# Linear attention's last stage: the norms of three heads moved beside the fourth head's products

## The chip, the cores and the metric

The kernel runs on one core of one Trainium2 chip. The metric is the time of one execution on the device, in microseconds (us); less is better. A core has five engines that run side by side and wait for each other by semaphores: TensorE (PE in the profile, with its weight loads apart as PEld), VectorE (DVE), ScalarE (ACT), GpSimd (POOL) and SyncE (SP), which here only issues the weight transfers. TensorE writes to PSUM, which has eight banks of 512 float32 columns; the other three work from PSUM or SBUF.

## The reference

Two transformer blocks over 512 latent tokens and 256 context tokens, width 1024. The change concerns the first block's gated linear attention (GLA): 4 heads, key width 64, value width 128. What the stage at hand has to compute, from the reference:

```python
def merge_outputs(o_ret, o_gla, p, ret_norm_w, gla_norm_w, w_out, dtype):
    ...
    gl = merge_heads(o_gla * lax.rsqrt(jnp.mean(o_gla * o_gla, axis=-1, keepdims=True) + EPS))
    gl = gl * gla_norm_w * jax.nn.silu(p[7].astype(jnp.float32))
    return jnp.concatenate([r, gl], axis=-1).astype(dtype) @ w_out
```

Here `o_gla` is the sum of a forward and a backward scan. In the kernel each head's output is a product of its values with a 512 x 512 matrix of scores (the "own" products), plus a product of its decayed queries with the states that the context leaves behind (the "state" products), one for each direction. The rows of `w_out` that belong to GLA are applied after it, and the result is added to the residual `x` with a gate. The norm of the second feed-forward part follows.

## The kernel before

Everything is float32, laid out with features on the 128 partitions and tokens on the columns. Large products against weights are made in three passes: a weight is split into a high part `wh` (ScalarE, line 385) and a low part `wl` (VectorE, line 393), an activation likewise, and the passes high x high, high x low and low x high are added in PSUM. A float32 product without that split goes through TensorE in two passes, so one `matmul` of these shows as two records.

Each engine has its own instruction list, written out by hand in functions with the engine's name at their end (`gla_pe`, `gla_act`, `gla_dve`, `gla_pool`), and works through it in order. A `signal` is a counting semaphore: `.up(key)` goes with the instruction that raises it, `.at(key)` with the one that waits. `empty(pe, b)` makes TensorE wait until the last reader of bank b, noted in `emptied`, is done.

The end of the GLA stage, in the order of TensorE:

- Line 2149: the far parts of the score matrices, two bank halves for each head; ScalarE copies each into `W` (line 2258, printed `g_W`), in the order of the heads.
- `own_pe(h)`, line 2077: four products of 512 columns (eight passes) into bank 4+h, for heads 0 and 1 with the transposes of the decayed keys (line 2161) between them, then the context states (line 2171, banks 2 and 3; ScalarE copies them, line 2271), then heads 2 and 3. Before the first one TensorE waits for the last of ScalarE's copies into `W`.
- Line 2182: the state products of heads 0 to 3, two a head, contracting over 64 rows. Heads 0 and 2 lie on partitions 0 to 63, heads 1 and 3 on 64 to 127. They end the sum in bank 4+h and raise `gla_head`.
- ScalarE squares bank 4+h (line 2274, `g_sq`), then VectorE scales it by the norm's weight and the gate `gg` (line 2321, `g_g`).
- Line 2192: sums of the squares over features, as products with one column, four for each head (eight records), all 16 columns of the result in bank 0. Filler products (`idle_products`, line 473) whose result nobody reads stand between.
- One column step for all heads: mean plus epsilon (VectorE, line 2324), root (ScalarE, line 2277), reciprocal (VectorE, line 2326), then for each head a block of diagonal matrices of the factors (VectorE, line 2330, `g_dg`).
- Line 2200: a product with ones spreads each head's factors over the partitions, into bank h; four filler products follow.
- For each head VectorE multiplies by the factors (line 2334), ScalarE copies the product into the high part `gy` (line 2280, `g_y`), and the low part `gyl` (`g_yl`) is made by VectorE for heads 0 and 2 (line 2337) and by GpSimd for heads 1 and 3 (line 2351).
- `outproj_pe` with `by_features`, line 447: four chunks of `w_out`, each 256 output features from the 4 heads, 24 passes a chunk, banks 0 and 1 or 3 and 4. TensorE waits once for the low parts of heads 2 and 3. Within a chunk the first 128 output features come first, then the others. VectorE adds each half to `x` (line 1173), ScalarE squares it for the next norm (line 510), and both split the weights of the chunk after next between them.

The SyncE queue's transfers for this stage were issued before it, up to one at 966.85 us, and the next follows at 1032.41 us.

Of the kernel before, what the change touches and what calls it, by code (L numbers as in the profile page):

```python
# [6 lines left out]
EPS = 1e-6  # L7
# [233 lines left out]
def build(nc, wts, vec, con, conds, xin, cin, cin2, out):  # L241
# [5 lines left out]
    F32, F32R = mybir.dt.float32, mybir.dt.float32r  # L247
    ACT = mybir.ActivationFunctionType
    MUL, ADD, SUB, MAX, MIN = ALU.mult, ALU.add, ALU.subtract, ALU.max, ALU.min
# [60 lines left out]
    ones, ident, blk64, perm = (con0[:, 128 * i:128 * i + 128] for i in range(4))  # L310

    def V(n, i=0, w=1):
        return vecs[:, VEC[n][0] + i:VEC[n][0] + i + w]

    bank = [stack.enter_context(nc.psum_tensor(f"ps{i}", [128, 512], F32)) for i in range(8)]
# [86 lines left out]
    emptied = [None] * 8  # L402

    def empty(pe, *banks):
        for b in banks:
            if emptied[b]:
                s, key = emptied[b]
                pe.wait_ge(*s.at(*key))
                emptied[b] = None
# [59 lines left out]
    def idle_products(pe, b, n):  # L469

        empty(pe, b)
        for _ in range(n):
            pe.matmul(bank[b][:, :], ones, con0[:, :], start=True, stop=True, skip_group_check=True)  # L473
# [1438 lines left out]
    gla_spread = signal("gla_spread")  # L1912
    gla_done = signal("gla_done")

    def outproj_pe(pe, name, k0, yh, yl, ready, ctx, key, between=None):
        for m in range(4):
            b = SETS[m % 2]
            if m == 0:
                ready(pe)
            by_features(pe, W_OF[name, k0, 256 * m], b, yh, yl, True, ctx)  # L1920
            for i in range(3 if ctx else 2):
                emptied[b[i]] = resid, (key, 0, m, i)
            if between:
                between(m)
# [27 lines left out]
    def tiles_of(t):  # L1952
        return t.rearrange("p (j n) -> p j n", j=4)
# [117 lines left out]
        emptied[6] = consumer, ("narrow", 0)  # L2071
        emptied[7] = consumer, ("narrow", C)

    def own_pe(pe, h):
        empty(pe, 4 + h)
        for jt in range(4):
            pe.matmul(bank[4 + h][:, :], gv[:, 2 + jt, 128 * h:128 * h + 128], W[:, h, jt, :], start=jt == 0, stop=False, skip_group_check=True)

    FAR = ((0, 1), (1, 0), (2, 3), (3, 2))

    def gla_pe(pe):
        narrow_pe(pe, w_in(GR), rank)
# [11 lines left out]
        def ready(pe):  # L2094
            pe.wait_ge(*y_low_pool.at("r", 3))
# [32 lines left out]
        for s in (7, 8):  # L2128
# [4 lines left out]
            for h in range(4):  # L2133
# [9 lines left out]
                else:  # L2143
                    for half in range(2):
# [5 lines left out]
                                          qq[:, 256 - 256 * half:512 - 256 * half], start=True, stop=True, skip_group_check=True)  # L2150
                        i.then_inc(*far.up(8, h, half))
                        emptied[bb] = far_out, (8, h, half)
        pe.wait_ge(*far_out.at(8, 3, 1))
        pe.wait_ge(*values_out.at("g", 5))
        own_pe(pe, 0)
        for d in range(2):
# [16 lines left out]
            i.then_inc(*gla_state.up(d))  # L2173
            emptied[bb] = gla_state_out, (d,)
        own_pe(pe, 2)
        own_pe(pe, 3)
        pe.wait_ge(*gla_state_out.at(1))
        pe.wait_ge(*query_decayed.at(1))
        for h in range(4):
            hp, r0 = h // 2, 64 * (h % 2)  # L2180
            for d in range(2):
                i = pe.matmul(bank[4 + h][:, :], stt[r0:r0 + 64, d, hp, 128 * (h % 2):128 * (h % 2) + 128], qs[d][r0:r0 + 64, hp, :],
                              start=False, stop=d == 1, skip_group_check=True)
            i.then_inc(*gla_head.up(h))
            emptied[4 + h] = gla_scaled, (h,)
        empty(pe, 0)
        for h in range(4):
            if h == 1 or h == 2:
                idle_products(pe, 1, 1)
            pe.wait_ge(*gla_sq.at(h))  # L2190
            for i in range(4):
                j = pe.matmul(bank[0][:, 4 * h + i:4 * h + i + 1], gsq[:, h, 128 * i:128 * i + 128], ones[:, 0:1], start=True, stop=True,
                              skip_group_check=True)
        j.then_inc(*sums_out.up("g"))
        emptied[0] = rstd, ("g", 0)
        idle_products(pe, 1, 1)
        for h in range(4):
            empty(pe, h)
            pe.wait_ge(*gla_diag.at(h))
            pe.matmul(bank[h][:, :], ones, gdg[:, 512 * h:512 * h + 512], start=True, stop=True,  # L2200
                      skip_group_check=True).then_inc(*gla_spread.up(h))
            emptied[h] = gla_done, (h,)
        idle_products(pe, 6, 4)

        def ready(pe):
            pe.wait_ge(*y_low.at("g", 2))
            pe.wait_ge(*y_low_pool.at("g", 3))

        outproj_pe(pe, "w_out", 4, Lat(gy), Lat(gyl), ready, False, "gla")

    def gla_act(act):

# [56 lines left out]
        for d in range(2):  # L2269
            act.wait_ge(*gla_state.at(d))  # L2270
            act.activation(stt[:, d, :, :], bank[2 + d][:, :].rearrange("p (j n) -> p j n", j=2), ACT.Copy).then_inc(*gla_state_out.up(d))
        for h in range(4):
            act.wait_ge(*gla_head.at(h))
            act.activation(gsq[:, h, :], bank[4 + h][:, :], ACT.Square).then_inc(*gla_sq.up(h))
        c = cb[:, 0:3, :].rearrange("p a b -> p (a b)")[:, 0:16]
        act.wait_ge(*rstd.at("g", 0))
        act.activation(c, c, ACT.Sqrt).then_inc(*root.up("g"))
        for h in range(4):
            act.wait_ge(*gla_done.at(h))
            act.activation(gy[:, h, :], gg[:, h, :], ACT.Copy).then_inc(*y_high.up("g", h))  # L2280

        outproj_act(act, "w_out", 4, lambda m: None, norm3, lambda e, k: e.wait_ge(*resid.at("gla", "x", k)))

    def gla_dve(dve):
# [31 lines left out]
        for d in range(2):  # L2316
            dve.wait_ge(*key_exp.at(d))
            dve.tensor_tensor(kx[:, d, :, :], kx[:, d, :, :], kk[:, :, CTX], MUL).then_inc(*key_decayed.up(d))
        for h in range(4):
            dve.wait_ge(*gla_sq.at(h))  # L2320
            dve.scalar_tensor_tensor(gg[:, h, :], bank[4 + h][:, :], V("gla_norm_w", h), gg[:, h, :], MUL, MUL).then_inc(*gla_scaled.up(h))
        c = cb[:, 0:3, :].rearrange("p a b -> p (a b)")[:, 0:16]
        dve.wait_ge(*sums_out.at("g"))
        dve.tensor_scalar(c, bank[0][:, 0:16], 1.0 / 128, EPS, MUL, ADD).then_inc(*rstd.up("g", 0))
        dve.wait_ge(*root.at("g"))
        dve.reciprocal(c, c).then_inc(*rstd.up("g"))
        dve.wait_ge(*rstd.last())
        shp = [128, 4, 128]
        for h in range(4):
            dve.tensor_tensor(tiles_of(gdg[:, 512 * h:512 * h + 512]), ident.unsqueeze(1).broadcast_to(shp),  # L2330
                              c[:, 4 * h:4 * h + 4].unsqueeze(2).broadcast_to(shp), MUL).then_inc(*gla_diag.up(h))
        for h in range(4):
            dve.wait_ge(*gla_spread.at(h))
            dve.tensor_tensor(gg[:, h, :], gg[:, h, :], bank[h][:, :], MUL).then_inc(*gla_done.up(h))
            if h % 2 == 0:
                dve.wait_ge(*y_high.at("g", h))
                dve.tensor_tensor(gyl[:, h, :], gg[:, h, :], gy[:, h, :].bitcast(F32), SUB).then_inc(*y_low.up("g", h))
        outproj_dve(dve, "w_out", 4, lambda k, s: M1[:, 40 + k, s:s + 1], False, "gla", lambda m: None, norm3)

    def gla_pool(pool):  # L2340
# [1703 lines left out]
```

## Time and profile before

| | us |
|---|---|
| median of 3 runs | 2681.16 |
| lowest and highest | 2677.81, 2688.44 |
| the profiled execution, its own time | 2678.36 |
| its span, first to last instruction | 2676.6 |

| engine | busy, share of the span |
|---|---|
| TensorE | 2590.9 us, 97% |
| VectorE | 1289.2 us, 48% |
| ScalarE | 820.4 us, 31% |
| GpSimd | 221.3 us, 8% |

The mean granted clock of TensorE over the span is 0.983 of full speed. The chain of work that ended last has 87% of its time on TensorE. The stage that the change touches lies between some 976 and 1029 us of the span. Busy shares here are shares of time in which a record of the engine is open; TensorE's matmuls overlap, so their starts tell the pace, and a busy TensorE may be doing fillers.

### The profile page before, as it was taken

The page shows a single profiled execution, that of the slowest core. Times are in us where ns is not written, and L with a number is a line of the kernel's source. Part 1 is how long each engine was busy: PE and PEld are TensorE (multiplying, and loading weights), DVE is VectorE, ACT ScalarE, POOL GpSimd, SP SyncE. Part 2 cuts the span into 40 slices and gives each one's busy share as a digit, 9 for nine tenths or more (in the row PEclk, how much of TensorE's full clock was granted, in tenths as well). Part 3 has the DMA queues.
Part 4 walks back from the last instruction along what each step waited for, and adds up shares of the span by engine and source line. Part 5 has one row for each costly group of instructions (what it writes and reads, how often), then busy time and mean ns, then how long its engine had stood idle before and what let it go on. Part 6 is the DMA issues. An engine that isn't in the chain of part 4 may idle for free.

```text
span 2676.6 us, 30609 instructions
## 1 busy us (share of the span) xinstructions
PE 2590.9 (97%) x12874; PEld 2039.6 (76%) x12874; DVE 1289.2 (48%) x1978; ACT 820.4 (31%) x1180; POOL 221.3 (8%) x176
## 2 busy tenths in 40 slices
PE   7999999999999999999999999999999999999998
PEld 4888888888756766888887686787788688686666
DVE  6564434336345745667647522522332342476562
ACT  3211112134333243222224313122222312245663
POOL 0100000021110000000000020110210011110001
PEclk9999999999999899999999999999999999999999
DMA  7344333312102002455532110110021011011010
GB/s 281 118 153 145 136 136 110 111 48 95 56 25 79 8 24 79 159 183 177 176 125 77 57 40 17 68 51 32 32 79 48 16 65 62 32 65 64 32 48 32
DMA packets 45401, 223.54 MB, mean 84 GB/s; under 512 B 4768, under 2 KB 6992, under 8 KB 30672
## 3 DMA queue, kind: packets, MB, share of 16 engines
q1 hardware_dynamic: 43296, 215.24, 22.8%
q10 hardware_dynamic: 1968, 6.34, 0.7%
q8 instruction: 102, 1.67, 0.2%
q14 instruction: 35, 0.29, 0.0%
HBM read 219.46 MB, written 2.10 MB: 83 GB/s over the span
## 4 chain that ended last, share of the span: by engine, by line
PE 87%; DVE 6%; ACT 4%; issue 2%; POOL 1%; DMA 0%; SPq 0%; POOLq 0%; DVEq 0%; ACTq 0%
PE ps L447 41%; PE ps L444 12%; PE ps L1513 7%; PE ps L422 3%; PE ps L3344 3%; PE ps L2892 3%; PE ps L867 1%; PE ps L1236 1%; PE ps L3552 1%; ACT wh L385 1%; PE ps L3456 1%; DVE wl L393 1%; PE ps L2710 1%; PE ps L3576 1%; PE ps L473 1%
## 5 line engine op out<-in xcount | busy, mean ns | idle before, releaser
L393 DVE TENSOR_TENSOR wl<-stage,wh 128x2048 fp32r<-128x2048 f32 (+2 forms) x157 | 326.2, 2078 | 633.1 <-ACT wh L385 632.9
L447 PE MATMUL ps<-hh,wh 128*128 128x512 f32 x1152 | 456.5, 396 | 0.0
L447 PE MATMUL ps<-hl,wh 128*128 128x512 f32 x1152 | 455.7, 396 | 0.0
L447 PE MATMUL ps<-hh,wl 128*128 128x512 f32 x1152 | 455.3, 395 | 0.0
L385 ACT ACTIVATE wh<-stage 128x2048 fp32r<-128x2048 f32 (+2 forms) x157 | 267.5, 1704 | 532.5 <-PE ps L447 387.0
L447 PEld LDWEIGHTS ps<-hh,wh 128*128 128x128 f32 x1152 | 217.8, 189 | 50.7 <-issue 1.2
L447 PEld LDWEIGHTS ps<-hh,wl 128*128 128x128 f32 x1152 | 217.4, 189 | 50.3
L447 PEld LDWEIGHTS ps<-hl,wh 128*128 128x128 f32 x1152 | 217.4, 189 | 49.1 <-issue 1.2
L641 DVE CUSTOM_DVE_ANT_0 left<-direct,cond_rows,vecs 128x1024 bf16<-128x1024 f32 x168 | 207.0, 1280 | 0.0
L444 PE MATMUL ps<-hh,wh 128*128 128x256 f32 x688 | 196.0, 285 | 4.0 <-DVE r_tb L1643 2.8
L444 PE MATMUL ps<-hh,wl 128*128 128x256 f32 x688 | 194.9, 283 | 0.0
L444 PE MATMUL ps<-hl,wh 128*128 128x256 f32 x688 | 193.8, 282 | 0.0
L444 PEld LDWEIGHTS ps<-hh,wh 128*128 128x128 f32 x688 | 131.9, 192 | 8.0 <-issue 4.3
L444 PEld LDWEIGHTS ps<-hl,wh 128*128 128x128 f32 x688 | 131.2, 191 | 0.0
L444 PEld LDWEIGHTS ps<-hh,wl 128*128 128x128 f32 x688 | 131.1, 191 | 0.0
L1513 PE MATMUL ps<-wh,hh 128*128 128x512 f32 x288 | 119.9, 416 | 0.0
L1513 PE MATMUL ps<-wh,hl 128*128 128x512 f32 x288 | 116.1, 403 | 0.0
L1513 PE MATMUL ps<-wl,hh 128*128 128x512 f32 x288 | 115.7, 402 | 0.0
L1191 POOL TENSOR_TENSOR ul<-sl,uh 128x768 fp32r<-128x768 f32 (+1 forms) x28 | 43.7, 1573 | 853.7 <-ACT uh L1082 853.4
L1082 ACT ACTIVATE uh<-sl 128x512 fp32r<-128x512 f32 (+1 forms) x42 | 30.8, 734 | 229.3 <-DVE sl L1142 138.2
L447 PE MATMUL ps<-uh,wh 128*128 128x512 f32 x240 | 94.3, 393 | 0.0
L447 PE MATMUL ps<-ul,wh 128*128 128x512 f32 x240 | 94.3, 393 | 0.0
(594 smaller groups left out, 4663.3 us busy)
## 6 DMA issues: line engine op xcount, KB each, us to landing
stage<-wts SPq DMA_DIRECT2D x108, 1024.0 KB, 4.8
direct<-wts SPq DMA_DIRECT2D x104, 512.0 KB, 4.2
stage<-wts SPq DMA_DIRECT2D x24, 768.0 KB, 4.3
stage<-wts SPq DMA_DIRECT2D x26, 512.0 KB, 3.3
group<-wts SPq DMA_DIRECT2D x6, 512.0 KB, 6.4
first<-wts SPq DMA_DIRECT2D x6, 512.0 KB, 9.7
x<-xin SPq DMA_DIRECT2D x4, 512.0 KB, 7.4
group<-wts SPq DMA_DIRECT2D x2, 1024.0 KB, 9.4
```

The source lines that it names most:

```text
L385: act.activation(split(m)[0][:, 0:w], stage[m % 2][:, 0:w], ACT.Copy).then_inc(*w_high.up(m))
L393: dve.tensor_tensor(l[:, 0:w], stage[m % 2][:, 0:w], h[:, 0:w].bitcast(F32), SUB).then_inc(*w_low.up(m))
L422: i = pe.matmul(bank[b[f]][:, :], w[:, k, 128 * f:128 * f + 128], s[:, k, LAT], start=k == 0 and a == 0, stop=k == nk - 1 and a == 2, skip ...
L444: i = pe.matmul(bank[b[2]][:, 256 * f:256 * f + 256], w[:, k, cols], s[:, k, CTX], start=st, stop=en, skip_group_check=True)
L447: i = pe.matmul(bank[b[f]][:, :], w[:, k, cols], s[:, k, LAT], start=st, stop=en, skip_group_check=True)
L473: pe.matmul(bank[b][:, :], ones, con0[:, :], start=True, stop=True, skip_group_check=True)
L641: dve.tensor_tensor_reduce(left[n % 2][:, :], chunk[:, :], rows_of[:, s, :], 1.0, bias[:, s:s + 1], MUL, ADD, to[:, s:s + 1]).then_inc(*mo ...
L1082: act.activation(z.uh[:, k, z.lo:T], z.sl[(2 * p + f) % 4][:, z.lo:T], ACT.Copy).then_inc(*u_high.up(n, p, f))
L1191: pool.tensor_tensor(z.ul[:, k, z.lo:T], z.sl[(2 * p + f) % 4][:, z.lo:T], z.uh[:, k, z.lo:T].bitcast(F32), SUB).then_inc(*u_low_pool.up(n ...
L1513: i = pe.matmul(bank[t][:, :], s[:, 4 * j + k, 128 * t:128 * t + 128], u[:, k, :], start=j == 0 and k == 0 and a == 0, stop=j == 1 and k = ...
L2892: pe.matmul(bank[b[0]][:, :], mv_[:, J, fs], wpart(J, C, T), start=J == 0, stop=J == 5, skip_group_check=True)
L3344: i = pe.matmul(bank[f][:, :], u[:, k, 128 * f:128 * f + 128], s[:, k, LAT], start=k == 0 and a == 0, stop=k == 7 and a == 2, skip_group_c ...
```

## The change

- `own_pe(0)` waits for ScalarE's copies into `W` of head 0, `own_pe(h)` for those of head h; the wait for head 3's ahead of all is gone. `own_pe` can be given some of its four products.
- State products of heads 0, 1 and 2 come right after the own products of head 2. Then two of head 3's four own products, the sums of heads 0 to 2 (bank 3), head 3's other two, its state products, the spread of head 0, the sums of head 3 (bank 2), the spreads of heads 1 and 2.
- The column step and the diagonals are done twice, for heads 0 to 2 and for head 3 (`NORM_HEADS`).
- A head's factors are spread into its own bank 4+h. All filler products of this stretch are gone.
- The first chunk of the projection uses the other branch of `by_features`: group k (head k's six passes, over both output halves) after a wait for the low part of head k. The spread of head 3 stands between groups 0 and 1. Both halves of the chunk are ready at its end.
- ScalarE's and VectorE's lists are put in the order that goes with it; head 0's product, high and low part stand in the middle of head 3's column step.

The diff:

```diff
-    def outproj_pe(pe, name, k0, yh, yl, ready, ctx, key, between=None):
+    def outproj_pe(pe, name, k0, yh, yl, ready, ctx, key, between=None, tile_ready=None):
         for m in range(4):
             b = SETS[m % 2]
-            if m == 0:
+            if m == 0 and ready:
                 ready(pe)
-            by_features(pe, W_OF[name, k0, 256 * m], b, yh, yl, True, ctx)
+            by_features(pe, W_OF[name, k0, 256 * m], b, yh, yl, True, ctx, tile_ready if m == 0 else None)
...
-    def own_pe(pe, h):
-        empty(pe, 4 + h)
-        for jt in range(4):
+    def own_pe(pe, h, jts=range(4)):
+        if jts[0] == 0:
+            pe.wait_ge(*far_out.at(8, h, 1))
+            empty(pe, 4 + h)
+        for jt in jts:
             pe.matmul(bank[4 + h][:, :], gv[:, 2 + jt, 128 * h:128 * h + 128], W[:, h, jt, :], start=jt == 0, stop=False, skip_group_check=True)
...
+    NORM_HEADS = ((0, 3), (3, 4))
...
-        pe.wait_ge(*far_out.at(8, 3, 1))
         pe.wait_ge(*values_out.at("g", 5))
         own_pe(pe, 0)
...
         own_pe(pe, 2)
-        own_pe(pe, 3)
         pe.wait_ge(*gla_state_out.at(1))
         pe.wait_ge(*query_decayed.at(1))
-        for h in range(4):
+
+        def from_states(h):
             hp, r0 = h // 2, 64 * (h % 2)
...
-        empty(pe, 0)
-        for h in range(4):
-            if h == 1 or h == 2:
-                idle_products(pe, 1, 1)
-            pe.wait_ge(*gla_sq.at(h))
-            for i in range(4):
-                j = pe.matmul(bank[0][:, 4 * h + i:4 * h + i + 1], gsq[:, h, 128 * i:128 * i + 128], ones[:, 0:1], start=True, stop=True,
-                              skip_group_check=True)
-        j.then_inc(*sums_out.up("g"))
-        emptied[0] = rstd, ("g", 0)
-        idle_products(pe, 1, 1)
-        for h in range(4):
-            empty(pe, h)
+
+        def sums(heads, n):
+
+            empty(pe, 3 - n)
+            for h in heads:
+                pe.wait_ge(*gla_sq.at(h))
+                for i in range(4):
+                    j = pe.matmul(bank[3 - n][:, 4 * h + i:4 * h + i + 1], gsq[:, h, 128 * i:128 * i + 128], ones[:, 0:1], start=True, stop=True,
+                                  skip_group_check=True)
+            j.then_inc(*sums_out.up("g", n))
+            emptied[3 - n] = rstd, ("g", n, 0)
+
+        def spread_head(h):
+
+            empty(pe, 4 + h)
             pe.wait_ge(*gla_diag.at(h))
-            pe.matmul(bank[h][:, :], ones, gdg[:, 512 * h:512 * h + 512], start=True, stop=True,
+            pe.matmul(bank[4 + h][:, :], ones, gdg[:, 512 * h:512 * h + 512], start=True, stop=True,
                       skip_group_check=True).then_inc(*gla_spread.up(h))
-            emptied[h] = gla_done, (h,)
-        idle_products(pe, 6, 4)
-
-        def ready(pe):
-            pe.wait_ge(*y_low.at("g", 2))
-            pe.wait_ge(*y_low_pool.at("g", 3))
-
-        outproj_pe(pe, "w_out", 4, Lat(gy), Lat(gyl), ready, False, "gla")
+            emptied[4 + h] = gla_done, (h,)
+
+
+        for h in range(3):
+            from_states(h)
+        own_pe(pe, 3, range(2))
+        sums(range(3), 0)
+        own_pe(pe, 3, range(2, 4))
+        from_states(3)
+        spread_head(0)
+        sums((3,), 1)
+        for h in (1, 2):
+            spread_head(h)
+
+        def tile_ready(c, k):
+            if c == 0 and k == 1:
+                spread_head(3)
+            pe.wait_ge(*(y_low_pool if k % 2 else y_low).at("g", k))
+
+        outproj_pe(pe, "w_out", 4, Lat(gy), Lat(gyl), None, False, "gla", None, tile_ready)
...
+        for n, (h0, h1) in enumerate(NORM_HEADS):
+            for h in range(h0, h1):
+                act.wait_ge(*gla_head.at(h))
+                act.activation(gsq[:, h, :], bank[4 + h][:, :], ACT.Square).then_inc(*gla_sq.up(h))
+            if n:
+                gla_high(0)
+            act.wait_ge(*rstd.at("g", n, 0))
+            act.activation(c[:, 4 * h0:4 * h1], c[:, 4 * h0:4 * h1], ACT.Sqrt).then_inc(*root.up("g", n))
+        for h in range(1, 4):
+            gla_high(h)
...
+        for n, (h0, h1) in enumerate(NORM_HEADS):
+            for h in range(h0, h1):
+                dve.wait_ge(*gla_sq.at(h))
+                dve.scalar_tensor_tensor(gg[:, h, :], bank[4 + h][:, :], V("gla_norm_w", h), gg[:, h, :], MUL, MUL).then_inc(*gla_scaled.up(h))
+            if n:
+                gla_done_dve(0)
+            cc = c[:, 4 * h0:4 * h1]
+            dve.wait_ge(*sums_out.at("g", n))
+            dve.tensor_scalar(cc, bank[3 - n][:, 4 * h0:4 * h1], 1.0 / 128, EPS, MUL, ADD).then_inc(*rstd.up("g", n, 0))
+            if n:
+                gla_low_dve(0)
+            dve.wait_ge(*root.at("g", n))
+            dve.reciprocal(cc, cc).then_inc(*rstd.up("g", n))
+            dve.wait_ge(*rstd.last())
+            for h in range(h0, h1):
+                dve.tensor_tensor(tiles_of(gdg[:, 512 * h:512 * h + 512]), ident.unsqueeze(1).broadcast_to(shp),
+                                  c[:, 4 * h:4 * h + 4].unsqueeze(2).broadcast_to(shp), MUL).then_inc(*gla_diag.up(h))
+        gla_done_dve(1)
+        gla_done_dve(2)
+        gla_low_dve(2)
+        gla_done_dve(3)
```

`gla_done_dve(h)` is line 2334's product (now from bank 4+h), `gla_low_dve(h)` line 2337's low part, `gla_high(h)` line 2280's copy; GpSimd's list is as it was.

## Rows read from the trace of the kernel before

**Rows 1.** The page's first line.

```profile
span 2676.6 us, 30609 instructions
```

**Rows 2.** The chain that ended last, 980 to 1040 us: start us, us, what.

```profile
980.75 0.61 ACT g_W L2258
...
1020.48 2.40 issue
1022.88 17.05 PE ps L447 x72
```

**Rows 3.** Timeline, TensorE and VectorE, 958 to 989 us: idle before in brackets.

```profile
976.00 4.71 PE L2149 MATMUL ps<-g_qs,g_qs 64*128 64x256 f32 x16 [2.26 <-ACT g_W L2258]
981.40 6.61 PE L2077 MATMUL ps<-g_W,g_v 128*128 128x512 f32 x8 [0.69 <-ACT g_W L2258]
...
981.89 1.29 DVE L2318 TENSOR_TENSOR g_kx<-g_kx,g_k 128x512 f32<-128x512 f32 x2 [8.77 <-ACT g_kx L2262]
```

**Rows 4.** Windows: us, PE, PEld, DVE, ACT, POOL busy, clock, DMA share, GB/s.

```profile
977.00:980.40 3.40, 3.40 (x13) 2.61 (x11) 0.00 (x0) 1.98 (x4) 0.00 (x0) 0.51 0.00 0
...
983.80:987.20 3.40, 3.40 (x5) 1.35 (x4) 0.00 (x0) 0.47 (x1) 3.40 (x2) 0.50 0.00 0
...
1007.80:1011.20 3.40, 3.40 (x25) 2.68 (x23) 0.54 (x1) 0.89 (x1) 0.00 (x0) 1.00 0.00 0
...
1018.00:1021.40 3.40, 2.48 (x6) 0.76 (x4) 2.08 (x3) 1.48 (x3) 1.26 (x1) 1.00 0.00 0
```

**Rows 5.** Timeline, TensorE and its weight loads, 992 to 1028 us.

```profile
995.61 7.03 PE L2077 MATMUL ps<-g_W,g_v 128*128 128x512 f32 x16
1002.57 3.81 PE L2182 MATMUL ps<-g_qs,g_st 64*128 64x512 f32 x16
...
1009.91 1.84 PE L2192 MATMUL ps<-con,g_sq 128*128 128x1 f32 x16
...
1003.53 0.20 PEld L2182 LDWEIGHTS ps<-g_qs,g_st 64*128 64x128 f32 x2 [0.23 <-issue]
```

**Rows 6.** Timeline, VectorE, ScalarE and GpSimd, 992 to 1028 us.

```profile
1004.59 1.09 ACT L2274 ACTIVATE g_sq<-ps 128x512 f32<-128x512 f32 x2 [8.18 <-PE ps L2182]
1005.22 1.41 DVE L2321 SCALAR_TENSOR_TENSOR g_g<-ps,vecs,g_g 128x512 f32<-128x512 f32 x2 [22.03 <-ACT g_sq L2274]
1007.41 1.28 ACT L2277 ACT_TABLE_LOAD   x1
1011.79 0.17 DVE L2324 TENSOR_SCALAR cb<-ps 128x16 f32<-128x16 f32 x1 [3.45 <-PE ps L2192]
1012.25 0.25 DVE L2326 RECIPROCAL cb<-cb 128x16 f32<-128x16 f32 x1 [0.28 <-ACT cb L2277]
1012.54 2.50 DVE L2330 TENSOR_TENSOR g_dg<-con,cb 128x512 f32<-128x512 f32 x4
1014.95 0.68 DVE L2334 TENSOR_TENSOR g_g<-g_g,ps 128x512 f32<-128x512 f32 x1
1015.67 0.63 ACT L2280 ACTIVATE g_y<-g_g 128x512 fp32r<-128x512 f32 x1 [3.45 <-DVE g_g L2334]
1016.33 0.69 DVE L2337 TENSOR_TENSOR g_yl<-g_g,g_y 128x512 fp32r<-128x512 f32 x1 [0.70 <-ACT g_y L2280]
1018.36 1.26 POOL L2351 TENSOR_TENSOR g_yl<-g_g,g_y 128x512 fp32r<-128x512 f32 x1 [30.30 <-ACT g_y L2280]
1018.91 1.26 DVE L2337 TENSOR_TENSOR g_yl<-g_g,g_y 128x512 fp32r<-128x512 f32 x1 [0.70 <-ACT g_y L2280]
...
1021.51 1.26 POOL L2351 TENSOR_TENSOR g_yl<-g_g,g_y 128x512 fp32r<-128x512 f32 x1 [1.89 <-ACT g_y L2280]
1026.73 0.63 ACT L510 ACTIVATE n_acc<-x 128x512 f32<-128x512 f32 x1 [5.30 <-DVE x L1173]
```

**Rows 7.** Timeline, ScalarE and VectorE, 1028 to 1042 us: the next weights' split.

```profile
1030.07 1.04 ACT L385 ACTIVATE wh<-stage 128x1024 fp32r<-128x1024 f32 x1
...
1031.15 1.23 DVE L393 TENSOR_TENSOR wl<-stage,wh 128x1024 fp32r<-128x1024 f32 x1 [0.26 <-ACT wh L385]
```

More of the change, by code:

```diff
@@ L2271, in gla_act, with gla_high @@
             act.activation(stt[:, d, :, :], bank[2 + d][:, :].rearrange("p (j n) -> p j n", j=2), ACT.Copy).then_inc(*gla_state_out.up(d))
-        for h in range(4):
-            act.wait_ge(*gla_head.at(h))
-            act.activation(gsq[:, h, :], bank[4 + h][:, :], ACT.Square).then_inc(*gla_sq.up(h))
         c = cb[:, 0:3, :].rearrange("p a b -> p (a b)")[:, 0:16]
-        act.wait_ge(*rstd.at("g", 0))
-        act.activation(c, c, ACT.Sqrt).then_inc(*root.up("g"))
-        for h in range(4):
+        def gla_high(h):
             act.wait_ge(*gla_done.at(h))
             act.activation(gy[:, h, :], gg[:, h, :], ACT.Copy).then_inc(*y_high.up("g", h))
+        for n, (h0, h1) in enumerate(NORM_HEADS):
[8 more added lines that the diff above has]
+            gla_high(h)
         outproj_act(act, "w_out", 4, lambda m: None, norm3, lambda e, k: e.wait_ge(*resid.at("gla", "x", k)))
@@ L2318, in gla_dve @@
             dve.tensor_tensor(kx[:, d, :, :], kx[:, d, :, :], kk[:, :, CTX], MUL).then_inc(*key_decayed.up(d))
-        for h in range(4):
-            dve.wait_ge(*gla_sq.at(h))
-            dve.scalar_tensor_tensor(gg[:, h, :], bank[4 + h][:, :], V("gla_norm_w", h), gg[:, h, :], MUL, MUL).then_inc(*gla_scaled.up(h))
         c = cb[:, 0:3, :].rearrange("p a b -> p (a b)")[:, 0:16]
-        dve.wait_ge(*sums_out.at("g"))
-        dve.tensor_scalar(c, bank[0][:, 0:16], 1.0 / 128, EPS, MUL, ADD).then_inc(*rstd.up("g", 0))
@@ L2325, in gla_dve, with gla_done_dve @@
-        dve.wait_ge(*root.at("g"))
-        dve.reciprocal(c, c).then_inc(*rstd.up("g"))
-        dve.wait_ge(*rstd.last())
         shp = [128, 4, 128]
[L2329 to L2332, printed above, removed]
+        def gla_done_dve(h):
             dve.wait_ge(*gla_spread.at(h))
[L2334 to L2337, printed above, removed]
+            dve.tensor_tensor(gg[:, h, :], gg[:, h, :], bank[4 + h][:, :], MUL).then_inc(*gla_done.up(h))
@@ new lines, in gla_low_dve @@
+        def gla_low_dve(h):
+            dve.wait_ge(*y_high.at("g", h))
+            dve.tensor_tensor(gyl[:, h, :], gg[:, h, :], gy[:, h, :].bitcast(F32), SUB).then_inc(*y_low.up("g", h))
+        for n, (h0, h1) in enumerate(NORM_HEADS):
[15 more added lines that the diff above has]
+                                  c[:, 4 * h:4 * h + 4].unsqueeze(2).broadcast_to(shp), MUL).then_inc(*gla_diag.up(h))
```

## The prediction

> **What bounds the kernel now.** First the page: one core, 2676.6 us of span, 2678.36 us as its own time (1.8 us lie around the span) [rows 1]. The median of the runs shown, 2681.16, is 2.8 us above the profiled execution. The change touches some 40 us, so I read only the end of linear attention: first the chain of work there, then TensorE alone, then the granted clock, then the other engines.
>
> The chain is TensorE nearly everywhere; what it does at the end, though, is not all work. After the last state product (from 1002.57) the projection starts at 1022.88 [rows 2, 5]. In these 20.3 us TensorE has 3.8 us of state products, 32 one-column sums, eight passes that spread the factors and seven filler products of two passes each that nobody reads. It then stands for 2.40 us before line 447 [rows 2]. The view calls that "issue", but VectorE's last product of head 3, ScalarE's copy and GpSimd's low part precede it, and the low part ends at 1021.51 + 1.26 = 1022.77 [rows 6]. So the bound is the dependent chain of head 3, not TensorE: the fillers are free time, and work put into it costs nothing.
>
> Unit prices on TensorE: a 512-column float32 pass goes off each 7.03/16, about 0.43 us, at full clock [rows 5], and each 0.85 at 1.2 GHz (6.61 us for eight, the last faster) [rows 3]. A one-column sum with its load takes 1.78/16, 0.11 us [rows 5]. A projection pass takes 17.05/72, 0.235 us, so a chunk of 24 takes 5.6 [rows 2]. Sixteen state passes took only 3.8 us, loads going in twos [rows 5]: heads 0 and 1, on rows 0 to 63 and 64 to 127, run beside each other, and so do 2 and 3. A pair costs 1.8 us; a head without its partner also costs 1.72 (four passes of 0.43).
>
> **The change part by part.** All times are those of before's trace, without the earlier start that the first part brings.
>
> *The wait ahead of the first own product.* It was for the last copy of head 3, 980.75 + 0.61, and the products began at 981.40 [rows 2, 3]. They now need head 0's copies only, long done. TensorE's last line-2149 pass ends at 980.7 and the next could go off at about 980.5, so they start 0.9 us earlier. The clock was at 1.2 GHz from 977 to past 987.2 [rows 4]. Had it come back at the same moment, the 0.9 us would be worth half, 0.45. Had it come back by 983.8 because the dense work starts earlier, 3.4 us more of it run at double pace: 0.9 + 1.7 = 2.6. If it comes back as long after the first product as before, the gain is 0.9, which I take. Nothing behind is in the way: VectorE's products for the transposes end at 981.89 + 1.29 = 983.2 [rows 3], and TensorE comes to them near 987.
>
> *The order of TensorE.* Head 2's own products start at 995.61 and take 3.4, to 999.1. Now head 3's eight follow only later. Heads 0 and 1 take their state products at 999.1 to 1000.95, head 2 alone to 1002.7. Then come four own passes of head 3 (1.7) to 1004.45, 24 sums of 0.11 (2.7) to 1007.2, four own passes to 1008.95, and head 3's state products alone to 1010.75. Splitting the pair 2 and 3 costs 1.7 us, and it stands on the path.
>
> *Norms of heads 0 to 2.* A square starts 2.0 us after its pair's first pass [rows 5, 6]: 1001.15, and head 2's at 1002.85, done 1003.45; VectorE's scalings of 0.75 follow. Both are ahead of the sums at 1004.45. The table load of 1.28 [rows 6], which stood under the sums, now starts at 1003.45 and is over by 1004.75, before the root at 1007.6. Sums out 1007.4, column step 0.17, root 0.2, reciprocal 0.25, diagonals of 0.6 each [rows 6]: head 0's factor is ready at 1008.7, head 2's at 1010. TensorE comes to head 0's at 1010.75, so all of it is hidden under head 3's products. That is what the change gains.
>
> *Head 3.* Its state products land 1.9 after their start, at 1010.9; square to 1011.5; TensorE spreads head 0 meanwhile (0.86) and then does eight sums, 1011.6 to 1012.5. VectorE has scaling (to 1012.2), head 0's product (to 1012.9), the column step, head 0's low part, which waits for ScalarE's copy of 0.63 (1013.6 to 1014.3), reciprocal (to 1014.5) and the diagonal (to 1015.2). Would the square after the root need a second table load? Line 510's square runs after the root and no load stands ahead of it [rows 6]; no. If it did, twice 1.28 at most.
>
> *The projection's inputs.* TensorE spreads heads 1 and 2 to 1014.25, and group k=0 (six passes, 1.4) starts with the low part of head 0, 1014.35 to 1015.75. Head 3's spread, ready since 1015.2, takes until 1016.6. VectorE's products of heads 1 and 2 end at 1015.8 and 1016.4. ScalarE's copy of head 1 ends at 1016.45, GpSimd's low part at 1017.8. So k=1 starts at 1017.9: a wait of 1.3 us on TensorE. Head 2's low part on VectorE, due at 1017.1 and behind it head 3's product, takes either 0.69 (as at 1016.33) or waits for GpSimd: the one that ran beside GpSimd's operation, at 1018.91, took 1.26 and ended 0.55 after it [rows 6]. I take the second, since it falls beside one here too: low part at 1018.35, head 3's product 1018.9, copy 1019.6, GpSimd's low part 1020.9. k=2 runs from 1019.3 to 1020.7, k=3 from 1021.0 to 1022.4. Before, the chunk ran 1022.88 + 5.6 = 1028.5. **Gain 6.1 us**; with the part ahead **7.0 us**. With the free low part (0.69) it would be 7.3.
>
> The Trainium skill (SBUF — State Buffer, "Who interferes with whom") says that a VectorE instruction with two SBUF inputs and a GpSimd instruction that reads SBUF shut each other out, the second waiting until the first has ended. The row at 1018.91 agrees (0.55 us after GpSimd's end), and by the rule the gain is the 7.0, not the 7.3. By it, too, an instruction of VectorE that came first would hold GpSimd's low part of head 1 back instead; VectorE's products of heads 1 to 3 have one input in PSUM and would not.
>
> *The loop order of the first chunk.* Both halves of the output now end with the chunk, not 2.8 us apart. Two additions of 0.75, two squares of 0.63, and the high part (1.04) and low part (1.23) of the chunk after next queue up behind it. Before, that low part ended at 1032.38, 3.9 after the chunk [rows 7]; I work out 4.8 now (additions to 1.8, second square to 2.4, high part to 3.5). The chunk between takes 5.6, so it is hidden with 0.8 us to spare. Were it not, only the excess would count.
>
> *Banks.* The spreads go into banks 4 to 7, free once the scalings are done (head 3's at 1012.2, spread at 1015.75); the sums into 3 and 2, which ScalarE has copied out before any state product starts. The fourteen fillers are gone, for which the clock is the only price.
>
> The rest is bound by TensorE in the same order, so I pass the 7.0 us on whole: 2678.36 - 7.0 = 2671.4 against the profiled execution, 2681.16 - 7.0 = 2674.2 against the median. I take 2673.
>
> **The rivals.**
> *A, the forecast*: 0.62, 2673 us, on its own 2669 to 2677.
>
> *B, the clock falls in the sums.* The 24 one-column sums run together for 2.7 us, with no filler between. For: a stretch with 2.26 us of standing at 973.7 [rows 3] led to 1.2 GHz from 977 on [rows 4]. Against: at 1007.8 to 1011.2 two thirds were such sums, with fillers, and at 1018 to 1021.4 TensorE stood for 0.9 us, and the clock held [rows 4]. The price, if it falls at 1007.2 and stays some 10 us as at 977: eight passes of head 3 cost 0.43 more each (3.4), the spreads and k=0 some 1.5 on the path; 5 in all. Gain 2, so 2678. Chance 0.18.
> The Trainium skill (TensorE: Matmul & The Clock Gate, "A second HAM failure mode: psum-queue depth-cycling") tells of kernels whose TensorE stands briefly between groups that go around the banks, and whose clock therefore swings between its levels. That rule speaks for B; the rows at 1007.8 and 1018 have such short stops at full clock, so I leave B the minor case.
>
> *C, the clock returns earlier at the own products.* 2.6 in place of 0.9 for the first part: 2671. Chance 0.12.
>
> *D, head by head doesn't pay.* A late low part of head 1 (a GpSimd operation held back by 0.7, or VectorE's queue holding head 2's product behind a late diagonal) makes TensorE stand at k=1 and then at k=3, as it now does once. Each us late there costs one; with 3 us late 2676. Chance 0.05.
>
> *E, slower.* The clock falls in the sums and stays down through the whole projection, since k=0 to k=3 wait between groups. A chunk of 24 passes then takes 24 x 0.43 = 10.2 instead of 5.6; four cost 18.5 more, with B's 5 it is 23.5, minus 7: 2695. It becomes slower than before from 14 us at 1.2 GHz on, each costing half, and by over 0.5% from 41 us on. In this stage the longest such stretch was 10 us [rows 4], and the later chunks run with no wait. Chance 0.03.
>
> **How the numbers follow.** 0.5%, 13.4 us, is about what a measurement of this kernel can tell from no change: the three runs shown lie from 2677.81 to 2688.44. No case gains 13.4; A to D all lie within 0.5%. The scatter of the medians can add some 5 us to C or A, which gives faster 0.05; E gives slower 0.03; the rest, 0.92, is the same. The range reaches from C less the scatter, 2666, to B with it, 2682.
>
> **What would show it.** The first own product some 0.9 us sooner after the last line-2149 pass. Twenty-four one-column sums in a row with head 3's passes on both sides, and no fillers. From the start of head 2's own products to the start of the second chunk some 26.8 us instead of 32.9. A stop of about 1.3 us ahead of k=1, and VectorE's low part of head 2 near 1.2 us. The granted clock at full speed from 1007 to 1018 shows A; 1.2 GHz there shows B. I am wrong if head 3's diagonal is not ready behind k=0, if a second table load stands there, or if the chunk after next waits for its low part.

## The result, and the profile after

The changed kernel takes 2670.47 us (median of 20 runs, 2664.19 to 2679.4) against 2681.84 (20 runs, 2673.49 to 2690.83): a ratio of 0.996, 95% interval 0.9949 to 0.997, or 8 to 14 us less. In a second measurement (the run e10 below) it was 0.996 again (0.9948 to 0.9973). The forecast of 2673 is 2.5 us above this median; the gain worked out for it, 7.0 us, lies just under the interval. The profiled executions: 2669.46 us with a span of 2667.7, before 2678.36 with 2676.6.

What an execution does ahead of the stage varies more than the change is worth: the second run of line-2149 passes starts at 976.00 before, at 977.40 and 981.22 in two executions of the changed kernel, and at 971.19 in the run e1 below, with the same instructions ahead. So I compare stretches between marks, the first mark being that start. The **first stretch** goes from there to the start of head 2's own products, the **second** to the first pass of the projection's second chunk, the **third** to the first pass of the second feed-forward, and the **rest** to the end.

| us | first | second | third | rest | sum |
|---|---|---|---|---|---|
| before | 19.6 | 32.9 | 28.2 | 1619.9 | 1700.6 |
| after | 17.5 | 27.0 | 28.7 | 1617.0 | 1690.3 |
| forecast | 18.7 | 26.8 | 28.2 | 1619.9 | 1693.6 |

The timeline of the changed kernel, TensorE (answers to [rows 3, 5]; the own products are now line 2079, the sums 2195, the state products 2184, the spreads 2204; in the first chunk line 422 is the head-by-head branch, k=1 its six passes of head 1):

```profile
977.40 4.75 PE L2152 MATMUL ps<-g_qs,g_qs 64*128 64x256 f32 x16 [2.27 <-ACT g_W L2274]
982.08 5.24 PE L2079 MATMUL ps<-g_W,g_v 128*128 128x512 f32 x8
...
994.92 3.60 PE L2079 MATMUL ps<-g_W,g_v 128*128 128x512 f32 x8
998.45 3.70 PE L2184 MATMUL ps<-g_qs,g_st 64*128 64x512 f32 x12
1002.08 1.98 PE L2079 MATMUL ps<-g_W,g_v 128*128 128x512 f32 x4
1003.90 2.73 PE L2195 MATMUL ps<-con,g_sq 128*128 128x1 f32 x24
1006.50 1.96 PE L2079 MATMUL ps<-g_W,g_v 128*128 128x512 f32 x4
1008.39 1.98 PE L2184 MATMUL ps<-g_qs,g_st 64*128 64x512 f32 x4
...
1017.24 0.50 PE L422 MATMUL ps<-g_y,wh 128*128 128x512 f32 x1 [0.83 <-POOL g_yl L2388]
...
1021.92 0.40 PE L447 MATMUL ps<-g_y,wh 128*128 128x512 f32 x1
```

The own products no longer wait (no bracket), and take 5.24 us, not 6.61. The order from 994.92 on is the one forecast, each piece within 0.2 us. The one stop over 0.5 us is at k=1, for GpSimd, 0.83 us. The same kernel's windows (columns as in [rows 4]):

```profile
978.40:985.20 6.80, 6.80 (x17) 4.17 (x16) 1.29 (x2) 4.99 (x9) 0.35 (x1) 0.50 0.00 0
...
1003.80:1006.60 2.80, 2.80 (x26) 2.70 (x25) 0.00 (x0) 0.28 (x1) 0.00 (x0) 1.00 0.00 0
1006.60:1018.00 11.40, 10.57 (x34) 5.22 (x34) 7.90 (x15) 2.76 (x6) 1.26 (x1) 1.00 0.00 0
...
1043.20:1046.60 3.40, 3.40 (x6) 1.34 (x5) 2.79 (x5) 0.21 (x1) 0.00 (x0) 0.51 0.81 248
```

Beside the own products TensorE was at 1.2 GHz for 6.8 us, where before it stayed there from 977 to past 987.2 [rows 4]. It held 2.4 GHz through the sums and the first chunk. At norm 3 it fell for 3.4 us, which it had not done before; that is the 0.6 us by which the third stretch is longer. Over all fourteen traces the third stretch is 28.7 us in the nine that have this fall and 28.2 in the five that don't (before, e1, e4, e6, e11). The low parts, VectorE and GpSimd (answers to [rows 6]):

```profile
1015.92 1.26 POOL L2388 TENSOR_TENSOR g_yl<-g_g,g_y 128x512 fp32r<-128x512 f32 x1 [26.40 <-ACT g_y L2292]
1019.07 1.29 POOL L2388 TENSOR_TENSOR g_yl<-g_g,g_y 128x512 fp32r<-128x512 f32 x1 [1.89 <-ACT g_y L2292]
...
1016.47 1.26 DVE L2351 TENSOR_TENSOR g_yl<-g_g,g_y 128x512 fp32r<-128x512 f32 x1 [0.70 <-ACT g_y L2292]
```

Head 2's low part started 0.55 us after GpSimd's operation and took 1.26 us, as forecast. The Trainium skill (SBUF — State Buffer, "Who interferes with whom") has the second of the two wait for the end of the first; VectorE ended 0.55 us after GpSimd, as before. GpSimd's operations here read and write SBUF alone: in no trace does a row of it name `ps`.

### The profile page after: what moved, and what is told of

Same layout as the page of the kernel before. It is cut to its first block, busy times and chain, and to the rows that moved or that the text cites. A ratio compares the mean times of both kernels' runs of the same rounds, so it can differ in the third digit from the quotient of the medians.

```text
span 2667.7 us, 30589 instructions
## 1 busy us (share of the span) xinstructions
PE 2585.7 (97%) x12860; PEld 2036.5 (76%) x12860; DVE 1289.0 (48%) x1980; ACT 820.9 (31%) x1181; POOL 221.4 (8%) x176
## 4 chain that ended last, share of the span: by engine, by line
PE 87%; DVE 7%; ACT 4%; issue 2%; POOL 1%; DMA 0%; SPq 0%; POOLq 0%; DVEq 0%; ACTq 0%
PE ps L447 41%; PE ps L444 12%; PE ps L1513 7%; PE ps L422 3%; PE ps L3381 3%; PE ps L2929 3%; PE ps L867 1%; PE ps L3589 1%; PE ps L1236 1%; PE ps L3493 1%; PE ps L2747 1%; ACT wh L385 1%; PE ps L473 1%; PE ps L3613 1%; DVE wl L393 1%
```

## The experiments

All with one trace each; ratios are to the kernel before, of 8 to 12 executions against 30 to 36 of the kernel before in the same measurement, with 95% intervals.

| run | first | second | third | rest | ratio |
|---|---|---|---|---|---|
| e1, before + early start | 17.5 | 33.0 | 28.2 | 1619.1 | 0.9979 (0.9968 to 0.999) |
| e2, after, old wait | 19.6 | 28.6 | 28.7 | 1621.1 | 0.9995 (0.9985 to 1.0005) |
| e3, after, one wait for all | 17.5 | 33.8 | 28.7 | 1620.8 | 0.9998 (0.9986 to 1.0011) |
| e4, after + fillers | 17.5 | 28.7 | 28.2 | 1619.6 | 0.9974 (0.9962 to 0.9986) |
| e5, low parts swapped | 17.5 | 26.4 | 28.7 | 1617.9 | 0.9956 (0.9942 to 0.997) |
| e6, before, no fillers | 19.6 | 33.2 | 28.2 | 1620.4 | 1.0 (0.9988 to 1.0012) |
| e7, before + by head | 19.6 | 28.8 | 28.7 | 1624.2 | 0.999 (0.998 to 1.0) |
| e9, heads in pairs | 17.5 | 27.4 | 28.7 | 1623.6 | 0.9972 (0.9957 to 0.9986) |
| e10, after again | 17.5 | 27.0 | 28.7 | 1621.0 | 0.996 (0.9948 to 0.9973) |
| e11, one low part on GpSimd | 17.5 | 26.0 | 28.2 | 1625.6 | 0.9956 (0.994 to 0.9973) |
| e12, pairs, none on GpSimd | 17.5 | 24.7 | 28.7 | 1620.2 | 0.996 (0.9947 to 0.9974) |
| e13, e2 + fillers | 19.6 | 28.7 | 28.7 | 1627.1 | 0.9989 (0.9978 to 1.0001) |

**e1, the early start alone.**

```diff
     def own_pe(pe, h):
+        pe.wait_ge(*far_out.at(8, h, 1))
         empty(pe, 4 + h)
...
-        pe.wait_ge(*far_out.at(8, 3, 1))
```

> The kernel before, with only the first part of the change: each head's own products wait for that head's copies. Two stretches are compared: the first from the second run of line-2149 passes to the start of head 2's own products (before 19.6 us, after the change 17.5), the second from there to the start of the projection's second chunk (before 32.9, after 27.0). Theory 1 (the start alone, clock as it falls): own products 0.9 us earlier, first stretch 18.7 on average over the clock's moments, the time 0.9 us shorter. Theory 2 (the earlier start regularly brings the clock back sooner): first stretch 17.5, the time 2.1 shorter. Both: second stretch unchanged at 32.9.

First stretch 17.5: theory 2. The own products of head 0 after it, at 1.2 GHz for 6.8 us:

```profile
972.80:979.60 6.80, 6.80 (x14) 3.30 (x11) 1.29 (x2) 4.90 (x8) 1.56 (x1) 0.50 0.00 0
979.60:983.00 3.40, 3.40 (x15) 1.97 (x14) 0.00 (x0) 1.08 (x2) 3.10 (x2) 0.99 0.00 0
```

In all nine traces with the early start this stretch is 17.5 us, in all five without it 19.6. The time was 3 to 9 us shorter, more than the 2.1 of theory 2; the section on the prediction comes back to that.

The second stretch stayed at 33.0 although the clock fell in it, which it had not done before. All fillers were in place, and the stop ahead of the spreads was the 0.65 us that before has too. Timeline and window:

```profile
1006.50 5.37 PE L2200 MATMUL ps<-g_dg,con 128*128 128x512 f32 x8 [0.65 <-DVE g_dg L2330]
...
1016.07 0.47 PE L447 MATMUL ps<-g_y,wh 128*128 128x512 f32 x1 [0.77 <-issue]
```

```profile
1007.00:1010.40 3.40, 3.40 (x5) 1.35 (x4) 2.70 (x5) 0.63 (x1) 0.00 (x0) 0.50 0.00 0
```

It cost nothing, because TensorE waits at the end of this stretch: its stop ahead of line 447 was 0.77 us in place of 2.40.

**e2, the changed kernel with the old wait.**

```diff
+        pe.wait_ge(*far_out.at(8, 3, 1))
         pe.wait_ge(*values_out.at("g", 5))
         own_pe(pe, 0)
```

> The changed kernel with the old wait put back: TensorE waits for ScalarE's last copy of head 3 ahead of the first own product. Theory 1: first stretch longer by 0.9 than with the change, 18.4 to 19.6 by the clock's moment; the time 0.9 longer than the changed kernel's. Theory 2: first stretch back at 19.6, 2.1 longer. Both: second stretch 27.0 as with the change.

First stretch back at 19.6, but the second is 28.6, which neither theory had. The timeline and the windows of this run:

```profile
1005.76 2.73 PE L2196 MATMUL ps<-con,g_sq 128*128 128x1 f32 x24
1008.36 3.08 PE L2079 MATMUL ps<-g_W,g_v 128*128 128x512 f32 x4
```

```profile
1005.60:1009.10 3.50, 3.50 (x27) 3.06 (x26) 0.29 (x2) 0.56 (x2) 0.00 (x0) 1.00 0.00 0
1009.10:1012.50 3.40, 3.40 (x5) 0.96 (x4) 2.00 (x4) 0.00 (x0) 0.00 (x0) 0.50 0.00 0
```

The clock fell for 3.4 us behind the 24 sums: rival B's mechanism, at 1.6 us. In the changed kernel it did not in either trace, nor in e3, e5 and e11, which have the same 24 sums and the early start. What differs in e2 is the wait ahead of the own products and, with it, when the clock had last risen.

**e13, e2 with fillers among the sums**, to see whether the sums did it.

```diff
             for h in heads:
+                if h == 1 or h == 2:
+                    idle_products(pe, 1, 1)
                 pe.wait_ge(*gla_sq.at(h))
```

> The changed kernel with the old wait (the run e2) and two filler products among the sums of heads 0 to 2. In e2 TensorE fell to 1.2 GHz at the end of the 24 sums and the second stretch took 28.6; in the changed kernel, with the earlier start, it did not and took 27.0. Theory 4 (the fall comes from sums without a filler at that moment): no fall here, second stretch 27.0 + 1.7 = 28.7, the time about that of e2. Rival (the fall has another cause): a fall again and 30.3. First stretch 19.6.

28.7 and no fall, over the same windows:

```profile
1005.60:1009.10 3.50, 3.50 (x22) 2.54 (x21) 0.00 (x0) 0.17 (x1) 0.00 (x0) 1.00 0.00 0
1009.10:1012.50 3.40, 3.40 (x15) 1.92 (x14) 2.11 (x5) 0.21 (x1) 0.00 (x0) 1.00 0.00 0
```

The forecast of theory 4 came true: with fillers among the sums, no fall. Theory 4 is still not the whole rule: e1 has fillers among its sums and fell at 1007.0, the changed kernel has none and did not. Each side of this comparison is one trace, and the fillers also move all that follows by 1.7 us. Fillers cost what the fall costs (1.7 against 1.6).

**e4, the changed kernel with the same fillers.**

> The changed kernel with two filler products (four passes) put back among the sums of heads 0 to 2. If TensorE is what bounds this part, as forecast: second stretch 27.0 + 1.9 = 28.9. If what follows has slack there: 27.0. If the clock sometimes falls without them, this kernel is the steadier one.

28.7: TensorE is on the path here, and with the early start there was no fall for them to prevent.

**e6, the kernel before without fillers**: the seven products of `idle_products` in this stretch taken out.

> The kernel before without the seven filler products of this stretch. If the fillers were free and the clock holds without them: the two among the sums stood on the path (about 0.97 us each), the others did not, so the second stretch is 32.9 - 1.9 = 31.0 and the time 1.9 shorter. If they held the clock up (the mechanism of rival B): 1.2 GHz somewhere between the sums and the first chunk, second stretch 33 or more.

33.2, the second case. The clock was at 1.2 GHz twice, behind the 32 sums and at the first chunk:

```profile
1009.20:1012.60 3.40, 3.04 (x4) 1.51 (x5) 2.70 (x5) 0.24 (x1) 0.00 (x0) 0.50 0.00 0
1019.40:1022.80 3.40, 3.24 (x8) 2.59 (x9) 0.00 (x0) 0.00 (x0) 0.06 (x1) 0.51 0.00 0
```

The seven fillers of before together paid for themselves (32.9 with them). Which of them kept the clock up where isn't separated here.

**e7, the head-by-head projection alone**: `tile_ready` with its waits and the spreads in banks 4+h, put into the kernel before; the last four fillers out.

> The kernel before with the head-by-head projection, the heads' own banks for the factors and without the four last fillers; the order of the norms stays as it was. By the rows of before, k=0 starts at 1017.1, k=1 after GpSimd at 1019.7, k=3 at 1022.8, the second chunk at 1024.3 in place of 1028.5: second stretch 28.7, 4.2 of the 5.9 us. If instead the norms beside head 3 carry the gain: second stretch above 31. First stretch as before.

28.8: 4.2 of the 5.9 us. The other 1.8 come with two things at once: the norms beside head 3's products, and without the three fillers that e7 still has, of which the two among the sums stand on the path. e4 has the new order of the norms with these two fillers and takes 28.7. So with them in place the new order is worth 0.1 us against e7; it hides work, but it also pays 1.7 us for the split pair. The 1.8 come from the fillers that can go, and whether e7's order would keep 2.4 GHz without them no run shows; the order of before did not (e6).

**e3, the changed kernel with one wait for all low parts.**

```diff
+        spread_head(3)
...
-        outproj_pe(pe, "w_out", 4, Lat(gy), Lat(gyl), None, False, "gla", None, tile_ready)
+        outproj_pe(pe, "w_out", 4, Lat(gy), Lat(gyl), ready, False, "gla")
```

> The changed kernel, but the projection waits once for all four low parts and its first chunk takes the old loop order; head 3's spread stands ahead of it. The chunk then starts when GpSimd has made head 3's low part, about 1020.4 in the changed kernel's times, perhaps 0.3 sooner: second chunk 4 us later, second stretch 31 and the time 4 longer than the changed kernel's. If the head-by-head order is worth little: under 29.

33.8, 6.8 more, not 4, and 0.9 more than the kernel before. TensorE stood 4.60 us (timeline), the clock fell, and the chunk ran its first 5.7 us at 1.2 GHz (windows):

```profile
1017.97 0.77 PE L447 MATMUL ps<-g_y,wh 128*128 128x512 f32 x1 [4.60 <-issue]
```

```profile
1016.90:1023.70 6.80, 5.73 (x14) 4.50 (x15) 0.23 (x1) 0.00 (x0) 0.97 (x1) 0.50 0.00 0
```

At 2.4 GHz these 5.7 us would have taken about half, an estimate of 2.9 us less or 30.9, which is the 31 expected. So the norms beside head 3 gain nothing behind one wait without fillers, for two reasons: the wait itself, and the low clock that it brings. Fillers under this wait, as the kernel before had them, were not tried; by the estimate they might leave 2 us of gain.

**e5, low parts swapped**: VectorE makes those of heads 1 and 3, GpSimd those of 0 and 2.

> The changed kernel with the low parts given the other way round: heads 0 and 2 to GpSimd, heads 1 and 3 to VectorE. Theory (VectorE's queue and GpSimd's two low parts end the chain now): k=0 starts 0.5 later, k=1 has no wait, k=3 needs VectorE's 0.7 in place of GpSimd's 1.3: second chunk 1.1 us earlier, second stretch 25.9. Rival (TensorE's passes bound it, low parts have slack): 27.0 or, with the later k=0, 27.5.

26.4, half way. No wait at k=1, but TensorE stood for 0.49 us ahead of k=0, for GpSimd's low part of head 0, and VectorE's diagonal of head 3, which started under that operation, took 1.54 us in place of 0.69:

```profile
1014.63 1.26 POOL L2387 TENSOR_TENSOR g_yl<-g_g,g_y 128x512 fp32r<-128x512 f32 x1 [23.75 <-ACT g_y L2292]
...
1014.90 1.54 DVE L2367 TENSOR_TENSOR g_dg<-con,cb 128x512 f32<-128x512 f32 x1
```

**e11, only head 2's low part on GpSimd.**

> The changed kernel with the low parts of heads 0, 1 and 3 on VectorE and that of head 2 alone on GpSimd. Theory (the two waits of TensorE in the first chunk are GpSimd's 1.3 us): no wait at k=1, VectorE's diagonal and low part of head 0 undisturbed, second chunk at 25.9 in place of 27.0. Rival (VectorE becomes the bound): 26.5 or more. The time 1 us shorter than the changed kernel's, if the clock falls in the same places.

26.0, within 0.1 of what was worked out. The stop at k=1 was 0.23 us, for VectorE's low part, in place of 0.83.

**e9, heads 2 and 3 as a pair**: `NORM_HEADS` is ((0, 2), (2, 4)); three of head 3's four own products ahead of the sums of heads 0 and 1, one behind; the spreads of heads 2 and 3 between k=0 and k=1.

> The changed kernel with the norms split in twos: heads 0 and 1 beside head 3's own products, state products of heads 2 and 3 as a pair again, the spreads of heads 2 and 3 between k=0 and k=1. Theory (splitting the pair costs 1.7 us on the path): the pair's passes take 1.8 for both, second chunk 1.5 us earlier, second stretch 25.5. Rival (head 2's norm, now late, costs as much as the pair saves): 27 or more.

27.4. The clock fell between k=0 and k=1:

```profile
1010.70:1014.10 3.40, 3.40 (x8) 1.99 (x7) 1.32 (x3) 0.58 (x1) 1.82 (x1) 0.50 0.00 0
```

and GpSimd's low part of head 1, which started while VectorE's diagonals ran, took 1.82 us in place of 1.26; at k=3 TensorE stood 0.94 us for GpSimd again:

```profile
1010.76 1.29 DVE L2371 TENSOR_TENSOR g_dg<-con,cb 128x512 f32<-128x512 f32 x2
...
1011.36 1.82 POOL L2389 TENSOR_TENSOR g_yl<-g_g,g_y 128x512 fp32r<-128x512 f32 x1 [23.64 <-ACT g_y L2293]
```

**e12, e9 with all low parts on VectorE.**

> The kernel with norms in twos (the run e9), with all four low parts on VectorE. In e9 the second chunk came at 27.4 and not at 25.5, and TensorE was at 1.2 GHz for 3.4 us between k=0 and k=1. If the clock holds: 24.6. If it falls again in the same place: 26.5.

24.7, the best stage: no fall, and no stop over 0.5 us in the first chunk. In the chain the state products are two pairs of 1.9 us, where the changed kernel has 3.63 for three heads and 1.93 for the fourth:

```profile
996.47 1.92 PE ps L2184 x8
...
1003.81 1.93 PE ps L2184 x8
...
1011.55 1.76 PE ps L2204 x4
1013.32 4.45 PE ps L422 x18
1017.76 2.34 PE ps L447 x10
```

Its ratio, 0.996, doesn't tell it from the changed kernel's: 2.3 us are less than the intervals. Against e9 only the low parts differ, against the changed kernel the pairs too.

**e10, the changed kernel again.**

> The changed kernel once more, unchanged, for a second trace. So far its trace took 73.3 us from the second run of line-2149 passes to the first pass of the second feed-forward (before 80.7), and 1617.0 from there to the end (before 1619.9; the same work). Theory 3 (where the clock falls later hangs on where this stage ends, so it repeats): the second part again about 3 us shorter than before's. Rival (chance of a single execution): anywhere between 1616 and 1624. Both: first stretch 17.5, second 27.0.

The three stretches repeat within 0.1 us, the rest doesn't: 1621.0 against 1617.0. Theory 3, that it repeats in each execution, is refuted. What is true of the mean is said below.

## Why the prediction was right, and where a term was off

- *What bounds the stage*: right. Behind the sums the dependent chain of head 3 was the bound, and the four fillers there were cover in it. But "the fillers are free time" was wrong in two ways. The two among the sums stood on the path, for 1.7 us (e4), and all seven together did something: e6 shows that without them the order of before loses 0.3 us, where their absence should have gained 1.9.
- *The wait ahead of the own products*: the mechanism was right, the size was not. I took 0.9 us; it gave 2.1 in every trace. A third of it is the earlier start (own products 4.68 us after the mark, not 5.40); the rest is that TensorE was back at 2.4 GHz after 6.8 us, not 10.2, so that head 0's eight passes took 5.24 and not 6.61. My upper bound had it as rival C, with 2.6 us and a chance of 0.12; C was what happened, with 0.7 and 1.4 for its 0.9 and 1.7. In e1 the own products start 4.08 us after the mark and take 5.86, with the same sum; the gain is 2.1 either way.
- *The order, the norms and head 3*: forecast 6.1, measured 5.9. Splitting the pair cost what I said, 1.7: the chain has 3.63 and 1.93 us of state products, e12's has 1.92 and 1.93. So the norms beside head 3 had to hide 1.7 us before they gained anything, and by e7 and e4 that is about all they did; the net gain of this part needs the fillers gone.
- *The projection by head*: right, and e7 gives it 4.2 us by itself. The stop at k=1 was 0.83 instead of 1.3: GpSimd was done when I said, counted from head 2's own products (22.3 us), and TensorE came to it 0.5 later than I said.
- *The loop order of the first chunk*: hidden, as forecast. The chunk after next had its low part 4.5 us after the first chunk (1025.17 + 1.22 in the timeline, second chunk at 1021.92); the chunk between took its usual time, and all later chunks kept their distance (16.6 us from the second chunk's first pass to the last).
- *Rival B*: not in the changed kernel, but a fall in or behind this stretch is real (e1, e2, e3, e6, e9). Behind the 24 sums its price was 1.6 us (e2), not 5, as the clock came back after 3.4 us. Of the two rows that I held against B only the one at 1018 has a stop; in the window from 1007.8 TensorE was busy for all 3.40 us. So 0.18 for B rested on one row less than I said.
- *Rival D*: a late low part of head 1 costs its full length only if nothing else is late; e11 took most of it away (0.83 to 0.23) and gained 1.0 us in all.
- *The rest of the program*: I passed the stage's gain on whole. The stage gave 7.4 (2.1 + 5.9 - 0.6 at norm 3). That the sum came so near the 7.0 is in part luck: 1.2 too little at the own products, 0.2 too much behind them, and a loss at norm 3 that wasn't in it. The profiled executions differ by 8.9, the medians by 11.4, and the interval begins at 8. So some 1 to 6 us come from elsewhere. One trace a kernel can't tell where: the rest after the stage took 1617.0 and 1621.0 in two traces of the same kernel, 1619.9 in the one of before, and 1617.0 to 1627.1 over all.

The span and the mean granted clock that are on record for each execution say more. TensorE runs at one of two levels, so the span times (1 - mean clock) is half of the time at 1.2 GHz, roughly what the low clock costs; the span times the mean clock is roughly the time without that cost. (Roughly, because low clock under a wait costs nothing.) Means in us:

| kernel | executions | span | span x clock | half of the time at 1.2 GHz |
|---|---|---|---|---|
| before, with the experiments | 97 | 2679.3 | 2628.8 | 50.5 |
| changed, both measurements | 31 | 2669.4 | 2622.6 | 46.9 |
| e1, early start | 12 | 2675.1 | 2628.7 | 46.4 |
| e2, old wait | 12 | 2678.0 | 2621.7 | 56.2 |
| e7, by head | 12 | 2677.4 | 2623.8 | 53.6 |
| e12, pairs | 12 | 2667.4 | 2620.1 | 47.3 |

Their standard errors are 0.2 to 0.5 us for the fourth column, and for the fifth 0.4 for before, 0.8 for the changed kernel and 1.0 to 1.5 for the others. The changed kernel gains 6.2 us apart from the clock and 3.7 by the clock: it spends some 7 us less at 1.2 GHz. In the traces of the three stretches both kernels spend 10.2 us there (before from 977 to 987.3 in one piece, after 6.8 us and, at norm 3, 3.4). So the saving lies outside them, and since the work ahead of the stage is the same, I put it down to what follows. e2 is 9 us slower than the changed kernel, and all of it is in the last column; 3.4 us of that are in the stage. e1's whole gain, 4 us, is in the last column too. Why TensorE spends less time at 1.2 GHz behind one end of the stage than behind another **stays open**.

The faster version to take on is e12: its stage is 2.3 us shorter than the changed kernel's, and its span times clock 2.5 us less, though its ratio does not show it faster.

## What to carry to other kernels

Where an engine waits on a chain of small steps through others, give its next consumer its inputs piece by piece before making the chain shorter: here that alone was 4.2 of 5.9 us, and the shorter chain behind one wait, without fillers, gained nothing. A wait on the last of several producers, where the first would do, costs its length and can cost more by the clock that comes back later: here 0.7 us and 1.4 us. Price filler products by what the clock does without them, in the very kernel, not by what they hide behind. And split a difference of whole executions by the mean granted clock before giving it to the stage that was changed.

## What the runs showed of the hardware

- The same 24 one-column sums, 2.73 us in a row, left the clock up in the changed kernel (both traces), in e3, in e5 and in e11, and were followed by 1.2 GHz in e2, 1009.1 to 1012.5. What differed was the wait ahead of the own products, and when TensorE had last risen to 2.4 GHz: 18.7 us before the sums (985.2 to 1003.90) in the changed kernel, 17.2 (some 988.6 to 1005.76) in e2. That this is the reason is not shown. Fillers are no sure guard: in e1 the clock fell from 1007.0 to 1010.4 with fillers among the sums and only the stop of 0.65 us that before has too.
- Windows from the start to the mark, of e1 and of e10, whose instructions up to there are the same:

```profile
0.00:971.19 971.19, 931.56 (x4820) 752.23 (x4820) 497.24 (x641) 270.31 (x370) 69.83 (x54) 0.99 0.30 105
```

```profile
0.00:981.22 981.22, 941.98 (x4821) 758.42 (x4821) 497.51 (x641) 270.36 (x370) 69.86 (x54) 0.98 0.29 104
```

TensorE is busy 10.4 us longer for the same work at a lower mean clock, while the other engines' busy times agree within 0.3 us. The clock records of the two traces have 20.5 us at 1.2 GHz in four stretches in e1 and 41.0 us in seven in e10; half of the difference is 10.2 us, and the mark lies 10.0 us later. Ten us ahead of the stage is as much as the whole change brings. The same shows in the scatter: over the 97 executions of before the span has a standard deviation of 3.9 us, the span times the mean clock one of 1.7.
- VectorE's operation with two SBUF inputs beside one of GpSimd's took 1.26 and 1.54 us instead of 0.69, when it started second, and ended 0.55 us after GpSimd's in all three cases (before, after, and e5: 1014.63 + 1.26 = 1015.89, 1014.90 + 1.54 = 1016.44). In e9, where VectorE had started first, it was GpSimd's that grew, by 0.56.
